# Second attention's end: the second sample group's turn and values moved forward, and part of the output projection begun earlier

## What is computed

```python
qp = b_query(xp, pos_p, norm_attn_b[j], w_q_b[j], qnorm_b[j])     # 3 dilation groups x 8 heads
for g, (win, dil) in enumerate(((128, 1), (512, 4), (2048, 16))):
    o_g, l_g = dilated_prompt(qp[:, :, g], kb_p, vb_p, dil, win // dil)
    o_g, l_g = dilated_sample(qs[:, :, g], k_ctx, v_ctx, dil, win // dil)
xp = xp + merge_groups(outs_p, lses_p).reshape(b, s, -1) @ w_o_b[j]
xs = xs + merge_groups(outs_s, lses_s).reshape(nb, ns, -1) @ w_o_b[j]
h = rmsnorm(tok, norm_ffn[l])
f = moe_ffn(h, w_router[l // 2], w_gu_moe[l // 2], w_down_moe[l // 2])   # top 2 of 8 experts
```

## Time and profile before

| what | us |
|---|---|
| median of three runs (1409.11 to 1409.96) | 1409.23 |
| the profiled execution | 1406.7 |
| its span, first to last instruction | 1405.0 |
| TensorE busy in the span | 1382.6 |
| VectorE, ScalarE, GpSimd busy | 463.3, 325.6, 173.9 |
| second attention and its output projection | about 452 to 510 |
| experts | from 524.77 |

### The profile page before, as it was taken

The page is one execution under the profiler, slowest core; times in us unless marked ns, Lnnn a source line. Parts: engine busy times, 40 slices in busy tenths (PEclk is TensorE's granted clock), DMA queues, the critical chain, the costliest instruction groups (busy, mean ns, idle before and its releaser), DMA issues.

```text
span 1405.0 us, 35284 instructions
## 1 busy us (share of the span) xinstructions
PE 1382.6 (98%) x15977; PEld 838.5 (60%) x15977; DVE 463.3 (33%) x981; ACT 325.6 (23%) x629; POOL 173.9 (12%) x218
## 2 busy tenths in 40 slices
PE   9999999999999899999999999999999999999998
PEld 7985999999998573363353353353354354344345
DVE  7977666664598640120120120120120120120121
ACT  6546644434454642001001001001001001001000
POOL 5623320000165611000000000000000000000100
PEclk9999999999999999999999999999999999999999
DMA  8959795535755279999999999999999999999994
GB/s 271 317 184 320 247 359 178 163 104 166 256 176 196 111 299 385 406 417 418 413 417 419 408 417 421 411 418 420 408 418 420 410 418 420 407 418 419 397 419 159
DMA packets 146426, 471.60 MB, mean 336 GB/s; under 512 B 9760, under 2 KB 81824, under 8 KB 117472
## 3 DMA queue, kind: packets, MB, share of 16 engines
q1 hardware_dynamic: 138544, 439.48, 79.9%
q0 software_dynamic: 7728, 29.82, 5.8%
HBM read 451.17 MB, written 18.09 MB: 334 GB/s over the span
## 4 chain that ended last, share of the span: by engine, by line
PE 95%; DVE 2%; ACT 1%; issue 1%; DMA 1%; SPq 0%; DVEq 0%; ACTq 0%
PE psum L1228 41%; PE psum L1268 21%; PE psum L369 9%; PE psum L370 9%; PE psum L371 9%; PE psum L937 1%; PE psum L922 1%; PE psum L962 1%; PE psum L1001 1%; DMA raw<-in_w_qkv_a 1%; PE psum L980 1%; DVE p_b L1713 0%; PE psum L872 0%; DVE wlo L365 0%; PE psum L861 0%
## 5 line engine op out<-in xcount | busy, mean ns | idle before, releaser
L1228 PE MATMUL psum<-wexp,xg 128*32 128x512 f32 (+1 forms) x6144 | 579.2, 539 | 0.0
L1228 PEld LDWEIGHTS psum<-wexp,xg 128*32 128x32 f32 x6144 | 199.4, 110 | 374.8 <-issue 373.3
L1268 PE MATMUL psum<-wexp,act 128*32 128x256 f32 x5376 | 291.5, 379 | 0.0
L2080 DVE TENSOR_TENSOR am<-sg,psum 128x512 f32<-128x512 f32 (+1 forms) x48 | 26.9, 616 | 731.5 <-issue 485.2
L1268 PEld LDWEIGHTS psum<-wexp,act 128*32 128x32 f32 x5376 | 174.7, 110 | 117.1 <-issue 3.1
L369 PE MATMUL psum<-hh,whi 128*128 128x288 f32 x696 | 207.3, 298 | 0.0
L370 PE MATMUL psum<-hl,whi 128*128 128x288 f32 x696 | 205.3, 295 | 0.0
L371 PE MATMUL psum<-hh,wlo 128*128 128x288 f32 x696 | 205.1, 295 | 0.0
L365 DVE TENSOR_TENSOR wlo<-raw,whi 128x2048 fp32r<-128x2048 f32 (+1 forms) x66 | 144.8, 2194 | 52.6 <-ACT whi L361 52.4
L369 PEld LDWEIGHTS psum<-hh,whi 128*128 128x128 f32 x696 | 130.8, 188 | 5.6 <-issue 3.7
L370 PEld LDWEIGHTS psum<-hl,whi 128*128 128x128 f32 x696 | 130.9, 188 | 0.1
(11 more groups left out here) (308 smaller groups left out, 1050.5 us busy)
## 6 DMA issues: line engine op xcount, KB each, us to landing
wexp<-in_w_moe SPq DMA_DIRECT2D x224, 1024.0 KB, 11.9
wexp<-in_w_moe SPq DMA_DIRECT2D x128, 768.0 KB, 11.2
raw<-in_w_gu_dense SPq DMA_DIRECT2D x22, 1024.0 KB, 5.2
wexp<-in_w_moe SPq DMA_DIRECT2D x32, 512.0 KB, 12.8
raw<-in_w_qkv_a SPq DMA_DIRECT2D x12, 1024.0 KB, 11.7
raw<-in_w_down_dense SPq DMA_DIRECT2D x16, 704.0 KB, 4.6
raw<-in_w_q_b SPq DMA_DIRECT2D x6, 1024.0 KB, 5.1
h_rows<-zeros POOLq DMA_DIRECT2D x14, 384.0 KB, 10.1
```

Source lines behind the costliest of these rows:

```text
L1228: ins = nc.tensor.matmul(ps[NG * part + r][32 * j:32 * j + 32, 0:wd], xg[:, r, 32 * k:32 * k + 32], wexp[:, q % RING, wd * j:wd * j + wd], ...
L1268: ins = nc.tensor.matmul(ps[6 + r // 2][32 * j:32 * j + 32, 256 * (r % 2):256 * (r % 2) + 256], act[:, r, 32 * kk:32 * kk + 32], wexp[:, q ...
L2080: V.tensor_tensor(am[:, r, 0:wd], sg[:, r, 0:wd], ps[NG + r][:, 0:wd], ALU.mult).then_inc(sem("gated_up"), 1)
```

## The change

It touches the second attention alone; for the first the calls stay as they are. On TensorE the turn of sample group 1 (job 5) goes ahead of the scores of pair 3. At the step after the last scores, the values of group 1 go ahead of the turns of jobs 6 and 7, the pick of group 1 follows these turns instead of standing a step later, and then come 18 matmuls of the projection: tiles 0 to 2, pairs 0 and 1. One step later, after the turn of job 9, come 9 more, tiles 0 to 2 with pair 2. The call of `residual` at the end makes the rest: pair 3 for tiles 0 to 2 and all pairs for tiles 3 to 7. On ScalarE the copy of a sample group goes ahead of the scaling of a pair's probabilities, and the scaling of group 1's output ahead of the copies of jobs 6 and 7, with its high part right behind them. On VectorE the low part of group 1 goes from behind job 9's sums to ahead of them.

```diff
@@ TensorE, attend
                 for t in range(n + lag + 2):
                     kind, i = unit_at(b, t)
+                    sample_first = ng > 1 and t == n - 1
+                    if sample_first:
+                        turn_probs(jobs_of(b, t - lag)[0], S_)
                     if kind == P_:
                         pair_scores(jobs_of(b, t), i)
...
                     if t == n and ng == 1:
-                        residual(P_WO, tiles_wo, "wo", b, True)
+                        residual(P_WO, tiles_wo, "wo", b, (0, nj - 4))
                     kind1, i1 = unit_at(b, t - lag)
-                    for k in jobs_of(b, t - lag)[0:1]:
+                    kind2, i2 = unit_at(b, t - lag - 1)
+                    if ng > 1 and t == n:
+                        sample_values(jobs_of(b, t - lag - 1)[0], i2)
+                        for k in jobs_of(b, t - lag):
+                            turn_probs(k, kind1)
+                        pick_rows(i2)
+                        residual(P_WOB, tiles_wob, "wob", b, (0, nj - 2))
+                        continue
+                    for k in jobs_of(b, t - lag)[0:1] if not sample_first else ():
                         turn_probs(k, kind1)
...
-                    if kind3 == S_:
+                    if kind3 == S_ and (ng == 1 or t < n):
                         pick_rows(i3)
                     for k in jobs_of(b, t - lag)[1:2]:
                         turn_probs(k, kind1)
+                    if ng > 1 and t == n + 1:
+                        residual(P_WOB, tiles_wob, "wob", b, (nj - 2, nj - 1))
@@ TensorE, residual
-            def residual(p0, tiles, tag, b, early=False):
+            def residual(p0, tiles, tag, b, early=None):
...
-                first = 4 * (groups - 1)
-                for m in range(2) if early else range(KD):
-                    if early:
+                ahead, first = (2, kn - 4) if b is A else (3, kn - 1)
+                for m in range(ahead) if early else range(KD):
+                    if early and b is A:
                         eng.wait_ge(sem(f"exped_{tg}"), exped_count(...))
+                    elif early:
+                        eng.wait_ge(sem(f"masked_{tg}"), max(masked_place(b, score_unit(b, k, g)) for k in range(len(b["jobs"])) for g in range(b["ng"])
+                                                             if score_bank(b, k, g) == m))
...
-                    for k in range(first) if early else range(first if m < 2 else 0, kn):
+                    for k in range(*early) if early else range(first if m < ahead else 0, kn):
@@ ScalarE, attend
                         before = jobs_of(b, t - 2)
+                        kind3, i3 = unit_at(b, t - 3)
+                        if t == len(b["units"]):
+                            scale_out(i3)
+                            for k in before:
+                                copy_job(k)
+                            sample_high(i3)
+                            continue
+                        samples = len(before) == 1
+                        for k in before if samples else ():
+                            copy_job(k)
                         for k in prompts[0:1]:
                             if k is not None:
                                 normalise(k, b["jobs"][k][1])
-                        for k in before[0:1]:
+                        for k in before[0:1] if not samples else ():
                             copy_job(k)
-                        if kind4 == S_:
+                        if kind4 == S_ and t < len(b["units"]):
                             sample_high(i4)
@@ VectorE, attend
                                 if k == b["vector_adds"][0] and low[0] == P_:
                                     prompt_low(low[1])
+                                    sample_low(unit_at(b, t - 3)[1])
...
-                        if kind4 == S_:
+                        if kind4 == S_ and t < len(b["units"]):
                             sample_low(i4)
```

More of the change, by code:

```diff
@@ L1027, in attend @@
                     if t == n and ng == 1:
-                        residual(P_WO, tiles_wo, "wo", b, True)
+                        residual(P_WO, tiles_wo, "wo", b, (0, nj - 4))
                     kind1, i1 = unit_at(b, t - lag)
-                    for k in jobs_of(b, t - lag)[0:1]:
+                    kind2, i2 = unit_at(b, t - lag - 1)
[7 more added lines that the diff above has]
+                    for k in jobs_of(b, t - lag)[0:1] if not sample_first else ():
                         turn_probs(k, kind1)
-                    kind2, i2 = unit_at(b, t - lag - 1)
                     if kind2 == P_:
```

## The result

The changed kernel is slower: a median of 1412.7 us in eight runs (1408.13 to 1416.28) against 1409.09 in eight of before, ratio 1.003 [1.0019, 1.0042]. The forecast of 1411.5 with 1408.9 to 1413.3 holds the time. But it gave the largest chance, 0.75, to a difference that the runs could not tell from none, and they tell it. (A ratio is the one measured with the runs, with its 95% interval; it is not the quotient of the two medians.) The same kernel, timed again in three other sets, gave 1.0018 [1.001, 1.0027], 1.0011 [1.0002, 1.002] and 1.0022 [1.0011, 1.0033]. Over all four sets its 43 runs have a mean of 1411.11 us; 121 runs of before, from the sets of the experiments, 1408.31. The difference is **2.80 us** (2.15 to 3.48 when the runs are drawn again at random), 0.20% of the time.

The account below looks back on a forecast made before the run. TensorE was taken to bound the kernel, with an unbroken expert run behind the change. Its waits rise from 5.54 to 7.81 us, so 1409.23 + 2.27 = 1411.5 us, range 1408.9 to 1413.3.

Parts of the forecast that it names:

- What bounds the kernel: Whole kernel: TensorE holds 95% of the last chain; experts wait for no load, so shifts before 524.77 reach the end.
- The walk: Second attention to its projection's end: queues followed instruction by instruction; TensorE's waits 7.81 us after, 5.54 before.
- +2.27: Predicted later end of the second attention's projection, in us: waits after minus waits before, bounds +1.2 to +3.4.
- The early projection: Between pick and turn 8: 18 matmuls wait 0.91 us, take 2.38 and hold turn 8 until 496.15.
- The last cached values are no term: Second group's values: their load, issued at 483.76, had landed by 488.03, so no wait was counted for it.
- A shift of this stretch is the same in both: Profiled execution (1406.7 us) and median (1409.23): the second attention's shift was added to the median unchanged.
- About what a measurement of this kernel can tell from none: Whole kernel time: a difference of 0.2%, 2.8 us, was taken as the limit of what runs can tell.
- same: Verdict on the whole kernel: no difference that the runs could tell, given a chance of 0.75.
- TensorE's clock falls: Rival, chance 0.05: clock drops to 1.2 GHz in the second attention's second pause; +4.7 to +8 us, 1414 to 1417.
- The clock is 1.00 inside a pause of 2.62: Argument against a clock drop: before, TensorE's granted clock stayed 1.00 in 486 to 488, inside its longest pause.
- The gain meets the loss: Rival, chance 0.15: VectorE's pace sets the masks, group 0's subtract keeps 487.71; +0.5 to +1.2 us, some 1410.1.
- The filling works: Rival, chance 0.05: early projection matmuls lie inside pauses, values start by about 486.5; -2.4 us, 1406.8.

Follow-up runs that it names:

- e6_after_again: The changed kernel timed again with no edit, in another set: median 1410.65 us, ratio 1.0018 to before; its profile has no clock fall in the stretch.
- e3_no_early: The changed kernel without the early projection, all 96 projection matmuls behind pair 3's values: 1409.46 us, ratio 1.0004 to before.
- e7_rearranged: Changed kernel reordered: job 5's turn back, group 0's high and low parts earlier, only 9 matmuls projected early, useless matmuls in pauses: 1407.76 us, ratio 1.0002 to before.
- e1_before_again: The kernel before, timed again with no edit: 1407.87 us.
- e14_turn_back_again: The changed kernel with job 5's turn back behind pair 3's scores, timed a second time in another set: 1414.38 us, ratio 1.0039 to before.
- e15_values_only: The changed kernel with job 5's turn back behind pair 3's scores and no early projection: 1409.79 us, ratio 1.0017 to before.
- e16_copy_first: The kernel before with one ScalarE edit, a sample group's copy ahead of the scaling of a pair's probabilities: 1409.08 us, ratio 1.0008 to before.
- e2_turn_back: The changed kernel with job 5's turn back behind pair 3's scores, all else as changed: 1412.58 us, ratio 1.0035 to before.

## Why the prediction was right, and where it was wrong

**What bounds the kernel** was right: the experts kept their 72.30 us, and all of the loss lies ahead of them.

**The walk** was right almost row for row. Starts of `e6_after_again` less 1.37 (476.12 - 474.75): scores at 482.88 (worked out 482.91), values of group 1 at 488.63 (488.74), turn 7 at 492.08 (492.17), early matmuls at 493.64 (493.77), turn 8 at 496.10 (496.15). From pair 2's low part on it is 0.2 to 0.7 late: the second piece starts at 498.71 instead of 498.48, the last part at 501.96 instead of 501.53. The end, 0.13 behind the start of the last matmul, is at 511.98 instead of 511.31, and the walk of before ended 0.37 early (509.04 for 509.41), so of the +2.27 the profile makes +2.57, within the 0.3 given for the method. VectorE and ScalarE did what was said. Their timelines, `e6_after_again`, against the earlier trace rows: first mask of pair 3, `sample_low` 0 and 1; copy 5 and the scaling behind it.

```profile
485.31 0.29 DVE L1739 CUSTOM_DVE_ANT_0 p_b<-psum,mask_b 128x128 f32<-128x128 f32 x1 [2.24 <-PE psum L922]
...
489.68 0.22 DVE L1807 TENSOR_TENSOR olo_b<-psum,ohi_b 128x64 fp32r<-128x64 f32 x1
...
494.64 0.22 DVE L1807 TENSOR_TENSOR olo_b<-psum,ohi_b 128x64 fp32r<-128x64 f32 x1 [2.02 <-ACT ohi_b L1426]
```

```profile
485.07 0.25 ACT L1386 ACTIVATE spn_b<-psum 32x128 f32<-32x128 f32 x1
...
488.03 0.40 ACT L1414 ACTIVATE p_b<-p_b,st_b 128x128 f32<-128x128 f32 x1 [2.45 <-DVE st_b L1753]
```

Mask at 483.94 on the time of before (483.97 worked out), `sample_low` 0 at 488.31 (488.40): copy 5 does fill ScalarE's wait, and the chain through VectorE ends later all the same.

**The early projection** was rightly named as ahead of the chain and not beside it. Taking it out gains 1.17 of the 2.57 (`e3_no_early`).

**"The last cached values are no term"** held for this order, where `sample_low` ends the wait. But the row proved only that they had landed by 488.03; they land at about 487.7 (`e7_rearranged`), so any order that starts the group's values before about 487.8 meets them. The rival that let the values start by 486.5 would have failed on this load also; the prediction saw VectorE alone.

**"A shift of this stretch is the same in both"** is the step that failed. The profiled execution of before took 1406.7 and the median 1409.23. The gap was read as a constant; the runs show that it goes with the clock: at a clock of 1.000 before takes 1406.43, and most executions lose some to falls. The stretch was costed at full clock and the shift carried over unchanged to executions that do not run at it; the loss to the clock was put at nothing. At full clock the difference is 2.25, as worked out. Where clock is lost it is 2.53 (at 0.998) to 3.75 (at 0.995). Over all runs it is 2.80, and 3.6 between the medians of the first set.

**"About what a measurement of this kernel can tell from none"**, said of 0.2%, failed with it. The intervals of the four sets reach only about 0.1% to either side, and in one of them a difference of 0.11% is told from none. The +2.27 itself is 0.16%. So "same" at 0.75 was too high even for the shift that was worked out; what the clock adds moved the result further from it.

**The rival "TensorE's clock falls"**, at 0.05, had the condition wrong and hit the size in part by luck. It gave 1414 to 1417, and the profiled execution, 1414.37, is such a one: +6.65 in the stretch, within +4.7 to +8. But the price was worked out for one fall in the second pause with all behind it up to turn 8 at half pace; the profile has three separate falls, the first behind the first pause, at 4.08 together. Nor is it an alternative to the forecast. Both happen, in different executions: 9 of 43 runs have a clock of 1.000, five are above 1414 with 0.994 or 0.995. Nor is there a point at a pause just above 2.62: the clock falls after pauses of 1.71, 2.03 and 0.78 in one execution and after none of the same pauses in another. "The clock is 1.00 inside a pause of 2.62" was true of one execution; `e1_before_again` shows the same kernel with 0.50 right behind that pause. The Trainium skill, "TensorE: Matmul & The Clock Gate", "HAM oscillation", speaks of pauses that send the engine back to half rate; the rows of after and of `e14_turn_back_again` agree that this happens here, at 0.50. What the page does not settle is the price of this change, which stays at 2.5 in stretches without any fall.

**"The gain meets the loss"** (1410.1) is refuted by the rows: `sample_low` 0 did not keep its 487.71. **"The filling works"** too: the early matmuls stand behind their own wait and ahead of turn 8.

**What stays open.** What decides in which execution the clock falls, and why it stays down for some 4 us in most places and for 10 to 17 in `e14_turn_back_again`, `e15_values_only` and `e16_copy_first`, the runs don't show. Nor do they show whether one long pause draws more falls than two shorter ones; the mean clocks (0.9951 in 11 runs of `e2_turn_back` and `e14_turn_back_again`, 0.9976 in 43 of after) hint at it. `e15_values_only`, with the same pause of 3.20, has 0.9958 in 12 runs; but `e16_copy_first`, whose longest pause in the stretch is 2.09, has 0.9960, which speaks against it.

## What to carry to other kernels

Work put into a pause helps only if it is beside the chain that sets the end: here 18 matmuls stood in front of the turn, copy and values that came last, and pushed them back by a little more than they saved (3.69 against 3.57). Walk each queue to the next late thing and ask of it what would be late after that (here a load that landed 0.9 earlier than it was needed). And where the profiled execution is faster than the median, find out what the other executions lose before carrying a shift over: a list of times with the granted clock beside each parts an order's cost from the clock's.

## What the runs showed of the hardware

The time of an execution lies roughly on a line with its mean granted clock: before from 1406.43 at 1.000 to 1410.87 at 0.995, after from 1408.68 to 1414.62. The falls stand where TensorE runs in bursts, in the second attention and in the router's part (16.8 to 17.1 us from the last projection matmul to the first expert with one, against 15.5 without), and none was seen in the run of the experts up to its last few microseconds. A fall's price depends on what is behind it: 0.52 where TensorE soon waits for another engine anyway, 1.4 to 1.5 where its work is on the path, and some 5 in `e14_turn_back_again`, where it lasted over the early projection (41.65 less the estimate of 36.6).
